# Norm-stage loads moved and weights in shares; choice of experts per tile and first expert loads paced, in a two-layer MoE block on one core

## The reference, cut to what matters

```python
def modulate(h, shift, scale):
    return h * (1 + scale) + shift

def moe(xf, router_w, router_b, w1, w3, w2, sw1, sw3, sw2):
    scores = jax.nn.sigmoid((xf @ router_w).astype(jnp.float32))
    _, idx = lax.top_k(scores + router_b.astype(jnp.float32), TOP_K)   # 6 of 64
    g = jnp.take_along_axis(scores, idx, axis=-1)
    g = g / (jnp.sum(g, axis=-1, keepdims=True) + 1e-20) * ROUTED_SCALE
    return routed_experts(xf, idx, g.astype(xf.dtype), w1, w3, w2) + swiglu(xf, sw1, sw3, sw2)
...
    for l in range(DEPTH):                                             # 2 layers
        sh1, sc1, gt1, sh2, sc2, gt2 = modulation(c, ada_w[l], ada_b[l])
        h = modulate(rms_norm(x, norm1_g[l]), sh1, sc1)                # and the same for the context hc
        y = even_mixer(h, ...)  or  odd_mixer(h, hc, ...)
        x = x + gt1 * y
        h2 = modulate(rms_norm(x, norm2_g[l]), sh2, sc2)
        x = x + gt2 * moe(h2, ...)
```

## Time and profile before

| what | us |
|---|---|
| median of three runs | 3269.23 |
| the profiled execution | 3287.37 |
| its span | 3285.6 |
| Modulation and what stands before it | 0 to 43.9 |
| NormIn(0) | 43.9 to 164.4 |
| MixOut(0) | 416.6 to 629.7 |
| Route(0), to the first expert matmul | 629.7 to 817.3 |
| Experts(0) | to 1683.3 |
| NormIn(1) | 1683.3 to 1833.1 |
| MixOut(1) | 2196.9 to 2342.1 |
| Route(1), to the first expert matmul | 2342.1 to 2490.8 |

### The profile page before, as it was taken

The page is one execution under the profiler, slowest core; times in us unless marked ns, Lnnn a source line. Parts: engine busy times, 40 slices in busy tenths (PEclk is TensorE's granted clock), DMA queues, the critical chain, the costliest instruction groups (busy, mean ns, idle before and its releaser), DMA issues. The chain is left out here.

```text
span 3285.6 us, 43943 instructions
## 1 busy us (share of the span) xinstructions
PE 2838.0 (86%) x12303; PEld 1228.7 (37%) x12304; DVE 1099.5 (33%) x1615; ACT 1156.8 (35%) x1310; POOL 1013.2 (31%) x964
## 2 busy tenths in 40 slices
PE   3999989865999999999929997779867999999991
PEld 1455534422333333333315544435422333333330
DVE  1322123411333333233325714533503333333334
ACT  1210101101565555455512004541113555555540
POOL 1000010062555554445510000000054555544453
PEclk7999999887999999999969999889888999999995
DMA  9330275251988888999655002013155999999965
GB/s 345 148 135 21 93 262 219 110 180 67 324 291 300 300 310 270 372 369 313 176 211 205 11 0 55 1 58 142 43 184 196 303 354 364 365 379 366 360 231 218
DMA packets 152846, 710.60 MB, mean 216 GB/s; under 512 B 38502, under 2 KB 39810, under 8 KB 96196
## 3 DMA queue, kind: packets, MB, share of 16 engines
q1 hardware_dynamic: 92020, 542.59, 41.8%
q0 software_dynamic: 58160, 157.64, 18.2%
q10 hardware_dynamic: 2592, 9.44, 0.8%
HBM read 623.60 MB, written 121.52 MB: 227 GB/s over the span
## 5 line engine op out<-in xcount | busy, mean ns | idle before, releaser
L1890 PE MATMUL ps<-arena,bc 128*64 x2224 | 990.2, 598 | 54.3 <-issue 20.6
L1891 PE MATMUL ps<-ht,bc 128*64 128x512 f32 x2224 | 990.4, 599 | 0.0
L1854 POOL DMA_INDIRECT bc<-h,kv x580 | 587.5, 1013 | 281.5 <-issue 178.7
L1961 ACT COPY ht<-arena 128x2048 f32 x282 | 521.8, 1897 | 160.6 <-issue 108.1
L1890 PE MATMUL ps<-arena,st 128*64 x1112 | 512.5, 605 | 26.9 <-issue 19.4
L1890 PEld LDWEIGHTS ps<-arena,bc 128*64 128x64 f32 x2224 | 296.1, 138 | 619.0 <-issue 616.7
L1891 PE MATMUL ps<-ht,st 128*64 128x512 f32 x1112 | 512.5, 605 | 0.0
L1984 DVE STREAM_TRANSPOSE bc<-bc 128x1024 f32<-128x1024 f32 x141 | 289.7, 2055 | 22.4 <-DMA bc<-h,kv 22.4
L1891 PEld LDWEIGHTS ps<-ht,bc 128*64 128x64 f32 x2224 | 296.2, 138 | 0.0
L1953 ACT COPY ht<-arena 128x2048 f32 x139 | 264.1, 1900 | 80.9 <-DMA arena<-exp_w_down 51.7
L1890 PEld LDWEIGHTS ps<-arena,st 128*64 128x64 f32 x1112 | 154.7, 140 | 348.8 <-issue 348.8
(11 more groups left out here) (253 smaller groups left out, 2952.7 us busy)
## 6 DMA issues: line engine op xcount, KB each, us to landing
arena<-exp_w_gate SPq DMA_DIRECT2D x128, 1024.0 KB
arena<-exp_w_up SPq DMA_DIRECT2D x128, 1024.0 KB
arena<-exp_w_down SPq DMA_DIRECT2D x128, 1024.0 KB
arena<-ada_w POOLq DMA_DIRECT2D x40, 1024.0 KB, 8.2
arena<-y SPq DMA_DIRECT2D x36, 512.0 KB, 15.2
xres<-st SPq DMA_DIRECT2D x28, 512.0 KB, 3.8
y<-gt SPq DMA_DIRECT2D x20, 512.0 KB, 5.7
bc<-h,kv POOLq DMA_INDIRECT x580
```

The source lines that it names most:

```text
L1854: g.indirect_dma_start(out=self.rows(parity)[:, c * 256:(c + 1) * 256], out_offset=None, in_=h2, in_offset=bass.IndirectOffsetOnAxis(ap=m. ...
L1890: te.matmul(out[0:UNIT], lhs[:, 0:UNIT], first, start=start, stop=stop)
L1891: return te.matmul(out[UNIT:P], lhs[:, UNIT:P], second, start=start, stop=stop)
L1961: a.copy(held[:, k], ring[:, k]).then_inc(self.held_gu, 1)
```

## The change: what it does

**Norm stages.** SP loads tiles 0 and 1 of x in Modulation, ahead of `ev_w_in`. ScalarE's queue takes the four `modrow` stores and, in both NormIn stages, the latent tokens' rows; SP loads the context tokens' rows behind tile 1, with a semaphore of their own that VectorE waits for at tile 8. The side steps start one tile later. `od_w_in` comes in three shares of 3 MB, issued by SP at the end of Experts(0), each as soon as the last rank that used its ring slot is done.

**MixOut.** ScalarE writes the sigmoid of a tile's logits where it copied them. VectorE chooses that tile's experts at once (`Choice.of_tile`), one tile per round from round 3 on, and one more after the loop.

**Route.** VectorE chooses for the last tile and releases the mask. TensorE makes the ranks right after the first gate_up. The places are picked before the pass tables are written (these release `tabled`, which SP waits for). ON_POOL is 1. Each early rank's loads wait for one more tile of y (`y_sb`). The first row lists, the first two blocks' gathers, the first transposition and the first copy out of the ring are made in Route.

```diff
@@ Modulation
+        for t in range(2):
+            self.norm.load_tile(sp, t)
         self.norm.load_weights(sp)
-        sp.wait_ge(self.ready, 1)
+    def act(self, act):
+        act.wait_ge(self.ready, 1)
         for s in range(4):
-            sp.dma_start(m.modrow[L, :, s * BANK:(s + 1) * BANK],
+            act.dma_start(m.modrow[L, :, s * BANK:(s + 1) * BANK],
@@ NormIn
+    def load_rows(self, eng, row, done):
+        if L:
+            eng.dma_start(m.gt[:, row * D:(row + 1) * D], bcast(m.modrow[0, row, 5 * D:6 * D])).then_inc(done, 16)
+        for i, seg in enumerate((1, 0)):
+            eng.dma_start(m.bc[:, (2 * row + i) * D:(2 * row + i + 1) * D],
+                          bcast(m.modrow[L, row, seg * D:(seg + 1) * D])).then_inc(done, 16)
...
             if t == 1:
-                if L:
-                    sp.dma_start(self.weights(), win).then_inc(self.wl, 16)
+                self.load_rows(sp, 1, self.mods_ctx)
...
+    def fetch_share(self, sp, i):
+        win = self.m.io["od_w_in"][0].rearrange("(p k) n -> p (k n)", k=KT)
+        part = slice(i * SLOT, (i + 1) * SLOT)
+        sp.dma_start(self.m.w[:, part], win[:, part]).then_inc(self.wl, 16)
...
     def act(self, act):
+        self.load_rows(act, 0, self.mods)
...
-                for i in range(self.SIDE_STEPS * t, min(self.SIDE_STEPS * (t + 1), self.side.steps)):
+                for i in range(self.SIDE_STEPS * max(t - 1, 0), min(self.SIDE_STEPS * t, self.side.steps)):
@@ MixOut
-                a.copy(m.logits[:, u, :], self.logit_bank(u)).then_inc(self.logit_out, 1)
+                a.activation(m.choice.score(u), self.logit_bank(u), ACT.Sigmoid).then_inc(self.logit_out, 1)
...
         for t in range(n + 1):
+            if t >= 3:
+                dve.wait_ge(self.logit_out, t - 2)
+                m.choice.of_tile(v, t - 3)
...
+        dve.wait_ge(self.logit_out, n - 1)
+        m.choice.of_tile(v, n - 2)
@@ Choice.of_tile, new (drains left out)
+        v.tensor_tensor(self.biased(t), self.score(t), self.small(self.BIAS, NE), ALU.add)
+        v.max(mx8, self.biased(t))
+        v.max_index(ix8, mx8, self.biased(t))
+        v.tensor_copy(ixf, ix8[:, 0:TOPK])
+        v.tensor_tensor(pairs(0), over(m.iota_e[:, :]),
+                        ixf.rearrange("p (k h) -> p k h", h=2).unsqueeze(3).broadcast_to([P, TOPK // 2, 2, NE]), ALU.is_equal)
+        v.tensor_tensor(both, slab[:, 0, t, :], slab[:, 1, t, :], ALU.add)
+        v.tensor_tensor(pairs(5), pairs(0), over(self.score(t)), ALU.mult)
+        v.tensor_tensor(both, both, slab[:, 2, t, :], ALU.add)
+        v.tensor_reduce(gate.rearrange("p (k h) -> p k h", h=2), pairs(5), AX.X, ALU.add)
+        mask = v.tensor_tensor(self.mask(t), both[:, 0:NE], both[:, NE:2 * NE], ALU.add)
+        v.tensor_reduce(total, gate, AX.X, ALU.add)
...
@@ Route
-    ON_POOL = 3
+    ON_POOL = 1
...
-        sp.wait_ge(self.placed, 1)
+        sp.wait_ge(self.tabled, 1)
...
         for r in range(EARLY):
+            sp.wait_ge(self.y_sb, n - 6 + r)
             expert = self.experts.expert(sp, r)
...
-            if t == 1:
+            if t == 0:
                 self.ranks(pe)
...
         h_out(n - 1)
+        act.wait_ge(self.regs_in, 16)
+        self.experts.hold(act, 0, 0)
         y_out(n - 1)
...
-        self.pass_tables(dve, pad, pend, filled, incl)
-        picked(mx(self.SEL, n * NE), self.GK)
+        for k in range(TOPK // 2):
+            v.tensor_tensor(pairs(5 + k), pairs(k), c.place(n).unsqueeze(2).broadcast_to([P, n, 2, NE]), ALU.mult)
+        for k in range(TOPK // 2):
+            v.tensor_reduce(at[:, :, 2 * k:2 * k + 2], pairs(5 + k), AX.X, ALU.add)
...
         v.scalar_tensor_tensor(dest, self.gt(self.GK, N), float(TABLE), row, ALU.mult, ALU.add).then_inc(self.placed, 1)
+        self.pass_tables(dve, pad, pend, filled, incl)
         for t in range(self.ON_POOL, n):
...
+        dve.wait_ge(self.table, 16)
+        self.experts.first_lists(dve)
@@ Experts.sync
+        if self.follower:
+            for i in range(self.follower.SHARES):
+                rank = NE - RING + (i - FIRST_SLOT[0] - NE) % RING
+                passes = sp.value_load(m.regs[0:1, 3 * P + rank:3 * P + rank + 1], min_val=1, max_val=self.nblk)
+                sp.wait_ge(self.down, passes + 1)
+                self.follower.fetch_share(sp, i)
```

More of the change, by code:

```diff
@@ L86, in __init__ @@
         self.rstd = sb("rstd", [P, NT])
[L88 removed]
+        self.choice = Choice(self)
         self.slots = sb("slots", [P, TABLE, 2], I32)
@@ L283, in __init__ @@
         self.hready, self.transposed, self.hta, self.htd = self.signals("norm", "hready transposed hta htd")
-        self.rows, self.rows_out = self.signals("in", "rows rows_out")
+        self.rows, self.rows_out, self.mods_ctx = self.signals("in", "rows rows_out mods_ctx")
         self.layer = layer
@@ L403, in dve @@
         m, v = self.m, self.nc.vector
-        dve.wait_ge(self.mods, 16 * (6 if self.layer else 4))
+        dve.wait_ge(self.mods, 16 * (3 if self.layer else 2))
         for t in range(NT + 1):
@@ L407, in dve @@
                 for q in range(1, 3):
-                    if self.SIDE_STEPS * (t - 1) == KT * q:
+                    if self.SIDE_STEPS * (t - 2) == KT * q:
                         self.side.take(dve, q)
+            if t == LT:
+                dve.wait_ge(self.mods_ctx, 16 * (3 if self.layer else 2))
             if t < NT:
@@ L451, in pe @@
                 if u == 0:
-                    pe.wait_ge(self.wl, 16)
+                    pe.wait_ge(self.wl, 48 if self.layer else 16)
                 pe.wait_ge(self.hta, u + 1)
@@ L828, in sync @@
                          bcast(m.modrow[L, row, 2 * D:3 * D])).then_inc(self.mods, 16)
+        sp.dma_start(m.choice.small(m.choice.BIAS, NE), bcast(io["router_b"][L])).then_inc(self.mods, 16)
         n = self.tiles
@@ L1525, in ranks @@
             for u in range(min(t + 1, n)):
-                last = te.matmul(out, m.before[:, :] if u == t else m.ones[:, :], mask[:, u * NE:(u + 1) * NE],
+                last = te.matmul(out, m.before[:, :] if u == t else m.ones[:, :], m.choice.mask(u),
                                  start=(u == 0), stop=(u == min(t, n - 1)))
@@ L1721, with __init__ @@
 class Experts(Stage):
-    def __init__(self, m, layer, tiles):
+    def __init__(self, m, layer, tiles, follower=None):
         super().__init__(m)
+        self.follower = follower
         self.index, self.x_t, self.gate_up = self.signals("moe", "index x_t gate_up")
@@ L1939, in gate, with hold @@
         return self.m.slots[:, ds(b, 1), 1:2].rearrange("p b c -> p (b c)").bitcast(F32)
+    def hold(self, act, b, parity):
+        m, a = self.m, self.nc.scalar
+        rank = self.rank(act, 1, b)
+        self.loaded(act, rank, self.w_gu, 32)
+        halves = lambda w: w.rearrange("p (h k n) -> p k h n", h=2, k=2)
+        ring, held = halves(m.arena[:, ds(self.at(rank), 2 * KT * DE)]), halves(self.held(parity))
+        for k in range(2):
+            a.copy(held[:, k], ring[:, k]).then_inc(self.held_gu, 1)
     def act(self, act):
@@ L1953, in hold_down @@
             a.copy(self.held_down(), m.arena[:, ds(self.at(rank) + 2 * KT * DE, 2 * D)]).then_inc(self.held_d, 1)
-        def hold(b, parity):
-            rank = self.rank(act, 1, b)
-            self.loaded(act, rank, self.w_gu, 32)
-            halves = lambda w: w.rearrange("p (h k n) -> p k h n", h=2, k=2)
-            ring, held = halves(m.arena[:, ds(self.at(rank), 2 * KT * DE)]), halves(self.held(parity))
-            for k in range(2):
-                a.copy(held[:, k], ring[:, k]).then_inc(self.held_gu, 1)
-        hold(0, 0)
         def body(b, parity, first):
@@ L2102, in build @@
         norm = [NormIn(m, 0), NormIn(m, 1)]
-        experts = [Experts(m, 0, NT), Experts(m, 1, LT)]
+        experts = [Experts(m, 0, NT, norm[1]), Experts(m, 1, LT)]
         out = [MixOut(m, 0, NT), MixOut(m, 1, LT)]
```

231 lines of the change are left out of this document (115 added, 116 removed).

## The result

The changed kernel takes 3256.0 us (median of six runs, 3251.0 to 3261.0), the kernel before, in its runs beside it, 3273.8: a ratio of 0.9953 (95% interval 0.9936 to 0.997). Forecast were 3163 us and a range from 3142 to 3212. It is faster, but by 15 us (the ratio; 18 between the medians) instead of 107. The profiled execution took 3260.98 us, 26.4 less than that of before.

A forecast was written before the change was run, and what follows sets the result against it. TensorE, busy for 86% of the span, was taken as the bound, so only its waits could be won. 10 + 17 + 54.8 + 39.9 less 15 gave 106.7 off 3287.4, less 18.1: 3163 us, range 3142 to 3212.

The forecast's parts named there:

- the term for the stalls: Route(0) and Route(1): late signals still cost 15 us for both layers, about 2 for each of eight rounds.
- Scatters alone, from 674 to 689, delayed nothing: Route(0): scatters without early expert loads beside them, at these times of the earlier trace, held no signal back.
- the copy on time at 2400.52: Route(1): ScalarE's copy after the first rank's loads were issued, read as one rank in flight causing no stall.
- the whole gain of pacing: Both Routes: loading each early rank only after another tile's y would leave 15 us of stalls.
- Rival 1: Both Routes: stalls stay while loads and scatters run together, in Route(0) from S (its start) + 64; 3201 us, chance 0.22.
- Route without stalls: Both Routes to the first expert matmul, counted without late signals: gains of 54.8 us in Route(0) and 39.9 in Route(1).
- the gain of 10: NormIn(0): an earlier stage start and fewer steps before the first product gain 10 us, bounds 0 to 14.
- the stores land some 4 us after issue: NormIn(0): modrow stores on ScalarE's queue land at about 35, so the stage starts 8 to 9 us earlier.
- the other half of that term: NormIn(0): a transposition and two steps fewer between the side step's weights and the first product, within the 10 us.
- NormIn(1): NormIn(1): loads on two queues and od_w_in loaded early gain 17 us, bounds 10 to 24.
- the 2.8 us taken: End of each MixOut: a later table load and a later choice cost 2.8 us per layer, bounds 0 to 6.

The follow-up runs named there:

- no_scatter: The changed kernel without the 60 and 48 scatters of routing entries, so its experts get no tokens; 3111 us in one run.
- no_pacing: The changed kernel without SP's four waits for y_sb ahead of the early expert loads; 0.9936 of the kernel before.
- scatter_gap: The changed kernel with a one-column memset on GpSimd after each scatter, nothing awaited; 0.9958 of the kernel before.
- tile_ev_six: The changed kernel with ev_w_in in 6 KB rows, twelve scatters meant at once, then six per tile of y; 3202 us, 0.9745 of the kernel before.
- before_four: The kernel before with its scatters in groups of four, each issued when the one before has landed; 0.9954 of the kernel before.

## Why the prediction was wrong

**The step that failed is the term for the stalls**, "I take 15 us for both layers". TensorE idled 75.3 us there (45.4 in Route(0), 29.9 in Route(1)), and against no_scatter its shared experts ended 50.6 and 36.7 us late, since the products that follow a stall are slower too (gate_up up to 8.5 us instead of 7.03). Under that term stands the sentence "Scatters alone, from 674 to 689, delayed nothing". That stretch ends too early: the train was 15 us old, and the first late signal was due after some 22. The loads began at the same time (689 to 697) and took the blame. In Route(1) the same reading fell in with it: the copy on time at 2400.52 stood 17 us into that train, so it was no evidence for one rank in flight. (The text calls the late down of the earlier trace rows that of tile 6; by its rows it is that of tile 4.) With the cause went the whole gain of pacing and, above all, the assumption that what the change does could avoid the stall. Rival 1 had it right that scatters stay and stalls stay, and still gave 3201, because it kept the loads as the stall's start, at S + 64. The stall starts at S + 47, 22 us after the first scatter, so two tiles fewer are through before it; it ends at S + 109, where the rival had 110, and the last turn_h comes at S + 164 instead of S + 143. It costs the same 45 us of TensorE as before, and since TensorE's shared expert sets the stage's end, an earlier table was worth nothing.

**Route without stalls was right in the middle and short at the end.** `placed` came at S + 24.1 (forecast 24.6; its terms add up to 24.4), TensorE's new wait was 5.23 us (3.5), and the shared expert ends at S + 119 to 120 in the stall-free kernels with the change (118). But the first expert matmul came 9 us behind the last gather and not 3 us. The last rows of GpSimd and the first of VectorE behind the barrier, in the changed kernel (timelines):

```profile
803.64 1.00 POOL L1908 DMA_INDIRECT bc<-h,kv  x1 [0.30 <-issue]
```

```profile
811.43 0.17 DVE L2043 COPY kv<-kv 128x5 int32<-128x5 int32 x1 [8.10 <-SPq L117]
```

GpSimd's drain at the barrier is the long one (duration min/median/max in ns):

```profile
L117 POOLq DRAIN  x30: 34/41/12372, 2.7 to 3257.9; - x30
```

It started at 797.9 and ended at 810.3, 5.6 us after the last gather's own row. The gathers that the change moved ahead of the barrier pay for that drain; before, they stood behind it.

**NormIn(0): the gain of 10 was 4.1 at the first product** (73.48 to 69.34). The stage started at 46.2 and not at 35, later than before, by the turns of 1.82 us above. The rule that the prediction cites from the Trainium skill, DMA: Bandwidth & Descriptors (Queues, rings and completion order), agrees with these records: the two queues take turns, packet by packet. But the step "the stores land some 4 us after issue" left out how long a turn is when the neighbour's packets are 48 KB. So GpSimd issued the side step's weights later and not 8 us earlier (46.49 against 44.13), and they landed at 67.35 against 66.11 (timeline of PE, changed kernel, as the earlier trace rows):

```profile
67.35 1.06 PE L825 MATMUL ps<-arena,cond 128*32 128x512 f32 x8 [1.55 <-DMA arena<-ada_w]
68.34 1.16 PE L554 MATMUL ps<-ident,arena 128*128 128x128 f32 x8
69.34 7.03 PE L545 MATMUL ps<-arena,ht 128*128 128x512 f32 x16
```

What gain there is comes from the other half of that term: only a step and a transposition (2.0 us) stand between the landing and the product, where before three steps and two transpositions did (7.4 us). The two differences, 5.4 less 1.2, are the 4.1.

**NormIn(1) was right.** VectorE starts 11.3 us into the stage (10), the first product has no wait and comes 30.9 us into it (29.8), and the stage gains 18.3 (17). Its end, as the earlier trace rows:

```profile
1798.37 7.07 PE L545 MATMUL ps<-arena,ht 128*128 128x256 f32 x32
1807.39 53.05 PE L1091 MATMUL ps<-ht,arena 128*128 128x512 f32 x123 [1.95 <-SPq L117]
```

It lasts from 1675.9 to 1807.4, before from 1683.3 to 1833.1. The three shares, issued from 1623.7 to 1644.4, cost Experts(0) nothing: it is 3.5 us shorter than before, which no run here explains.

**MixOut cost less than the 2.8 us taken**: 1.0 us in MixOut(0) (213.1 to 214.1) and 1.7 in MixOut(1) (145.2 to 147.0); the choice took 4.3 to 5 us a tile beside TensorE, as reckoned. The rest of the -7.9 is Attention, which the change does not touch: 203.6 us at a granted clock of 0.88, before 197.5 at 0.91. In `no_pacing`, whose Attention is the same, it took 196.6.

## What to carry to other kernels

Before a stall is put down to the thing that started just ahead of it, look for a second one that started earlier and ends with it: here the end of the stall told more than its beginning. It came 6.5 to 8 us after the last scatter in both layers, whatever the loads did. Check, too, that an experiment does what it was built for: the spacing in its own trace showed that scatter_gap had changed no rate and that tile_ev_six began with 24 scatters in a row, not 12. A train of small transfers can be broken by a wait on the work that it disturbs, and so regulates itself. On the second queue a small store paid one packet of its neighbour for its data and one for its signal, 1.82 us each with rows of 48 KB and about 0.3 with rows of 6 KB.

## What the runs showed that was not expected

- With GpSimd scattering at one per 1.275 us (128 entries of 8 bytes each) for 20 us and more, TensorE's signals reach the others up to 45 us after the matmuls' rows (692.3 to 737.4 in the changed kernel). ScalarE's and VectorE's own are prompt in the midst of the train: ScalarE's copy ends at 682.71 and VectorE starts at 682.73, VectorE ends at 683.15 and TensorE starts at 683.30. With groups of four, and one by one, there is no delay. During the train of the kernel before, most of SP's issues of loads take 0.70 us and stand 0.7 to 4.2 us apart within a rank; in before_four most take 0.34 to 0.54 and stand at most 1.2 us apart. What lies between the engines is not shown by the trace.
- The scatters themselves land in time: the last is followed by SP's read of the table after 1.2 us in the kernel before.
- GpSimd's drain lasts 5.6 us beyond the row of its last gather in Route(0) of the changed kernel.
